# Two plain column-group pairs instead of three ahead of the Strassen pairs, and the right-hand sums one pair earlier

## What is computed

```python
def rmsnorm(x, g):
    xf = x.astype(jnp.float32)
    y = xf * lax.rsqrt(jnp.mean(xf * xf, axis=-1, keepdims=True) + RMS_EPS)
    return (y * g.astype(jnp.float32)).astype(x.dtype)

def swiglu(x, wg, wu, wd):
    return (jax.nn.silu(x @ wg) * (x @ wu)) @ wd

    for l in range(DEPTH):          # DEPTH = 2
        x = x + 0.5 * swiglu(rmsnorm(x, ffn1_norm[l]), ffn1_wg[l], ffn1_wu[l], ffn1_wd[l])
        ...
        x = x + 0.5 * swiglu(rmsnorm(x, ffn2_norm[l]), ffn2_wg[l], ffn2_wu[l], ffn2_wd[l])
    return rmsnorm(x, final_norm)
```

## Time and profile before

| | |
|---|---|
| median of 3 executions | 1958.45 us (1956.9 to 1958.61) |
| the profiled execution, its own time | 1959.18 us |
| its span | 1957.4 us |
| TensorE busy | 1891.2 us (97%) |
| VectorE busy | 1348.5 us (69%) |
| ScalarE busy | 906.3 us (46%) |
| GpSimd busy | 243.1 us (12%) |
| mean granted clock of TensorE | 0.988 of full speed |

### The profile page before, as it was taken

How to read it: one execution, slowest core, us unless ns; L and a number is a source line. 1 busy time by engine, 2 the same in 40 slices (tenths; PEclk the granted TensorE clock), 3 DMA queues, 4 the chain that set the end, 5 groups by cost and what they waited for, 6 DMA issues and landing times.

```text
span 1957.4 us, 31136 instructions
## 1 busy us (share of the span) xinstructions
PE 1891.2 (97%) x11220; PEld 1654.4 (85%) x11220; DVE 1348.5 (69%) x1894; ACT 906.3 (46%) x1521; POOL 243.1 (12%) x208
## 2 busy tenths in 40 slices
PE   6999999998989999999999999999999999999996
PEld 5899988776868889998888999888776788999885
DVE  6789843566779579884357888525785677888424
ACT  4455523427347535553243555324377543555322
POOL 2100000213213210000021000001156221000001
PEclk9999999999989999999999999999999999999998
DMA  4232332322210222323222233332321022333321
GB/s 154 68 121 92 108 128 86 101 87 54 72 60 27 81 87 95 120 86 129 98 79 103 87 107 107 111 104 86 113 72 34 23 77 84 108 107 107 113 102 43
DMA packets 36204, 177.14 MB, mean 91 GB/s; under 512 B 12688, under 2 KB 13072, under 8 KB 15520
## 3 DMA queue, kind: packets, MB, share of 16 engines
q1 hardware_dynamic: 33696, 172.55, 26.0%
q10 hardware_dynamic: 2240, 2.98, 0.4%
q0 software_dynamic: 192, 0.59, 0.1%
HBM read 174.01 MB, written 2.10 MB: 90 GB/s over the span
## 4 chain that ended last, share of the span: by engine, by line
PE 90%; DVE 5%; ACT 2%; POOL 1%; issue 1%; DMA 0%; POOLq 0%; ACTq 0%; DVEq 0%
PE ps L308 29%; PE ps L310 28%; PE ps L309 28%; PE ps L1419 1%; DVE wl L278 1%; DVE xgl L356 1%; ACT wh L274 1%; PE ps L1442 1%; PE ps L1049 1%; POOL xg L2225 1%; DVE small L1005 0%; PE ps L1180 0%; PE ps L997 0%; POOL acc L390 0%; PE ps L979 0%
## 5 line engine op out<-in xcount | busy, mean ns | idle before, releaser
L308 PE MATMUL ps<-xgh,wh 128*128 128x256 f32 (+1 forms) x1504 | 514.7, 342 | 24.2 <-DVE xgl L356 13.8
L310 PE MATMUL ps<-xgh,wl 128*128 128x256 f32 (+1 forms) x1504 | 505.8, 336 | 0.0
L309 PE MATMUL ps<-xgl,wh 128*128 128x256 f32 (+1 forms) x1504 | 505.7, 336 | 0.0
L278 DVE TENSOR_TENSOR wl<-raw,wh 128x2048 fp32r<-128x2048 f32 (+1 forms) x93 | 215.0, 2312 | 355.6 <-ACT wh L274 355.6
L308 PE MATMUL ps<-tmh,wh 128*128 128x256 f32 (+1 forms) x1344 | 414.3, 308 | 0.0
L309 PE MATMUL ps<-tml,wh 128*128 128x256 f32 (+1 forms) x1344 | 414.3, 308 | 0.0
L310 PE MATMUL ps<-tmh,wl 128*128 128x256 f32 (+1 forms) x1344 | 414.3, 308 | 0.0
L274 ACT ACTIVATE wh<-raw 128x2048 fp32r<-128x2048 f32 (+1 forms) x93 | 176.5, 1897 | 356.6 <-PE ps L310 355.4
L308 PEld LDWEIGHTS ps<-xgh,wh 128*128 128x128 f32 x1504 | 286.8, 191 | 60.0 <-issue 18.9
L309 PEld LDWEIGHTS ps<-xgl,wh 128*128 128x128 f32 x1504 | 286.9, 191 | 30.4 <-issue 2.9
L310 PEld LDWEIGHTS ps<-xgh,wl 128*128 128x128 f32 x1504 | 286.6, 191 | 29.7
(11 more groups left out here) (284 smaller groups left out, 2599.8 us busy)
## 6 DMA issues: line engine op xcount, KB each, us to landing
raw<-in_units SPq DMA_DIRECT2D x161, 1024.0 KB, 4.9
x<-in_xT ACTq DMA_DIRECT2D x4, 512.0 KB, 7.7
outT<-x SPq DMA_DIRECT2D x8, 256.0 KB, 2.1
relb<-in_rpb SPq DMA_DIRECT2D x64, 24.0 KB, 2.2
cosA<-in_rope_a ACTq DMA_DIRECT2D x1, 256.0 KB, 2.6
sinA<-in_rope_a ACTq DMA_DIRECT2D x1, 256.0 KB, 2.9
cosD<-in_rope_d POOLq DMA_DIRECT2D x1, 256.0 KB, 3.2
sinD<-in_rope_d POOLq DMA_DIRECT2D x1, 256.0 KB, 3.0
```

Of the source, the lines that this page charges most:

```text
L278: nc.vector.tensor_tensor(wl[:, c % 2, 0:n], raw[:, c % 2, 0:n], wh[:, c % 2, 0:n].bitcast(F32), ALU.subtract).then_inc(w_lo, 1)
L308: nc.tensor.matmul(dst, lh, rh, start=first, stop=False, skip_group_check=onto)
L309: nc.tensor.matmul(dst, lh, rl, start=False, stop=False, skip_group_check=onto)
L310: return nc.tensor.matmul(dst, ll, rh, start=False, stop=last, skip_group_check=onto)
```

## The change

One less plain pair in each of the four blocks and one more pass of the Strassen loop; the four right-hand sums stand at the end of pair 0 in VectorE's queue. With `NS` = 2 the second pair (p == 1) is also the last plain one, so that `sums_hi`, `sums_lo` and the preparation of the first Strassen pair stand in the same pair.

```diff
@@ -47,7 +47,7 @@
-NS = 3
+NS = 2
 RP = PAIRS - NS
 HALF = SEQ // 2
@@ -766,7 +766,6 @@
                 if p == 1:
-                    right_sums(dve, f)
                     for t in range(4):
                         sums_lo(dve, f, t)
                 if p == NS - 1:
@@ -785,6 +784,7 @@
                 if p == 0:
                     for k in range(4, KD):
                         normed(k)
+                    right_sums(dve, f)
             right_lo(dve, f, 1)
```

## The result

The changed kernel takes 1979.24 us (median of 4, 1977.56 to 1980.09) against 1957.68 us of the kernel before (median of 4). The ratio is 1.0108, 95% interval 1.0095 to 1.0120: 1.1% slower. The forecast was 1978 us. The profiled execution has a span of 1978.2 us, 20.8 us more than before.

A forecast was written before the change was run, and what follows sets the result against it. TensorE was taken as the bound, waiting for VectorE's queue ahead of Strassen. 15.8 us lost in the blocks plus 2.8 for the clock made 18.6 on 1959.2, 1977.8; forecast 1978 us, 1976 to 1980, wider range 1970 to 1985.

The forecast's parts named there:

- The sum: Over the four blocks: 15.8 us lost net of the pass plus 2.8 us for TensorE's clock, 18.6 us in all.
- the blocks without the clock: From tg of pair 1 through the added pass: 3.1 us lost in block 1, 12.7 in the other three, together 15.8.
- the clock: TensorE at low clock from j=0 after the longer idle time: 0.7 us a block, 2.8 in all, range 0 to 9.4.
- The gain of the exchange: On TensorE, a Strassen pass of 20.16 us replaces a plain pair of 21.76: 1.60 us a block, 6.4 in all.
- VectorE's chain: VectorE's queue from tg of pair 1 to right_lo of part 1, second block: from 701.24, ending at 718.45.
- bounded at 0 to 0.9 and taken at 0.9: At sums_lo: GpSimd's two products with 1/rms hold VectorE back, starting 3.9 us after tg instead of 3.0.
- its old collision: In the kernel before, left_sum took 1.79 us beside GpSimd's work against 0.68; it was to lose these 1.1 us.
- the 3.4 us of the earlier trace: First block of the kernel before: after 3.86 us idle TensorE ran at half its granted clock for 3.4 us.
- The high bound: From j=0, the low clock lasting twice the row's stretch: 2.4 us a block, 9.4 in all.
- After that nothing is won back: After right_lo of part 1 the same queues follow as before, so the first pass wins back nothing.
- the forecast's rival with the shorter chain: Cover holds at right_lo of part 1: chain ending at 714.3 breaks even; full 6.4 us gain, 1952 to 1953; chance 0.05.

The follow-up runs named there:

- the pair of half changes: Two edits of the changed kernel: three plain pairs with only right_sums moved, 1958.06 us; two plain pairs with right_sums left where it was, 1978.63 us.
- the chain's two reorderings: Changed kernel with two sums_lo deferred behind right_lo of part 2, 1970.88 us; with left_lo of j=2 and j=3 also deferred behind right_lo of part 1, 1972.18 us.
- four plain pairs: Changed kernel with NS = 4 instead of 2, right_sums still at the end of pair 0: 1965.54 us, ratio 1.0034.
- the filled run: Changed kernel with five (first block) or six (others) never-read matmuls filling TensorE's idle time behind the last plain unit: 1973.74 us, ratio 1.0076.
- the run with the move alone: Changed kernel with NS back at 3, so only right_sums is moved to the end of pair 0: 1958.06 us, ratio 0.9995.
- the pieces: Kernel before with part 1 of xn in four pieces of 128x256, product j=1 waiting for one piece per row block: 1958.52 us, ratio 1.0001.
- the copy: Kernel before with part 1 of xn in four pieces and ScalarE's copy of product j=0 ahead of part 2 of xn: 1958.95 us, ratio 1.0005.
- the lightened pass: Kernel before with pieces and copy first, four left_sum of the first Strassen pass cut to 8 of 512 columns (computation incomplete): 1952.81 us, ratio 0.9975.
- the deferred sums: Changed kernel with two sums_lo behind right_lo of part 2, 1970.88 us; the same with two or three filling matmuls, 1973.01 us.
- four low parts deferred: Changed kernel with two sums_lo behind right_lo of part 2 and left_lo of j=2 and j=3 behind right_lo of part 1: 1972.18 us, ratio 1.0078.
- the run with the pairs alone: Changed kernel with right_sums put back behind tg of pair 1, still two plain pairs: 1978.63 us, ratio 1.0103.

## Why the prediction was right

**The place and the mechanism** are shown by the pair of half changes and by the chain's two reorderings: the loss is the missing pair, it sits in VectorE's queue, and two instructions taken out of that queue shorten TensorE's idle time by their 2.2 us. The sum came to 18.6 us and the profiled executions differ by 20.8. Three errors make that up: the blocks without the clock 0.9 us less than said, the clock 1.8 us more, and the mixers, which the sum did not have, 1.3 us more. That they partly cancel is luck.

**The gain of the exchange.** Worked out 1.60 us a block, measured 1.6 with four plain pairs. The figures of the Trainium skill ("TensorE: Matmul & The Clock Gate", "Back-to-back issue gap"), by which it would be 2.4 us, an estimate, or a loss, were left aside for the rows' 227 and 120 ns, and the run agrees with the rows.

**VectorE's chain.** From `tg` of pair 1 to j=0 the sum was 716.0 - 701.24 = 14.8 us; the changed kernel shows 722.70 - 707.98 = 14.72. `sums_lo` begins at 2.93 us and is held for 0.91 us, as bounded at 0 to 0.9 and taken at 0.9; the run without GpSimd's products confirms the cause. `left_sum` took 2.65 us, free of its old collision, as said. The idle time was to be 5.9 us and is 5.65. Without the clock the blocks lose 2.9, 4.0, 4.0 and 4.0 us (the filled run), 14.9 in all; the sum said 15.8.

**The clock** was the term with the wrong size, though small: 0.7 us a block was said, and the filled run puts it at 1.1, 1.3 and 1.6 us in the first three blocks and 0.6 in the fourth, 4.6 us instead of 2.8. (In the fourth the filled kernel is itself at the low clock for the last 3 us, granted 0.50 from 1957.8 on, and the changed one at 1.00, so 0.6 is too little.) The step that was off is the stretch. I took the 3.4 us of the earlier trace rows; in the changed kernel the steps of 0.21 us go on for 5.1, 4.9, 5.7 and 5.5 us in the four blocks (722.70 to the matmul at 727.55 in the second), so j=0 and nearly all of j=1 run slowly. The high bound, twice the row's stretch, held it. The row was one case of several: at the same place, behind nearly the same idle time (3.83 us against 3.86), the low clock lasted 5.8 us in the run with the move alone. A second small error had the other sign: a matmul of 256 columns costs 0.213 us at the low clock, not the doubled 0.24. From 120 ns for 256 columns and 227 for 512, 256 columns more cost 107 ns; 213 is twice that, and why the other 13 ns of the 120 do not appear beside it, no run here shows.

**"After that nothing is won back"** was right for the changed kernel, but for a reason that I had not worked out. I took the first pass as bound by TensorE, since the later passes are the earlier trace rows. It is bound by both: in the filled and the deferred kernels VectorE runs through it from `right_lo` to the third `tg` without a gap above 0.15 us, and the pieces, the copy and the lightened pass show the same limit in the kernel before. This is why the deferred orders end at 3.8 us a block, wherever the wait is put. In the forecast's rival with the shorter chain, an end at 714.3 that is reached by putting work later would therefore not have been enough to break even; no run here takes the work away from the chain altogether.

**What no step held**: the mixers. In the changed kernel's profile they moved by 2.6 and -1.3 us, together 1.3, and in the experiments of the table they lie between -1.0 and 2.6 (even) and between -2.5 and 0.0 (odd), with the time at the low clock. They fell out small here by chance.

## What to carry to other kernels

When a stage that feeds the next is shortened on the bound engine, add up what the other engines must finish under it, in the order of their queues, and compare the end with the new end of the stage; average shares (VectorE was at 69%) say nothing of that. A wait at such a border that vanishes in a timeline can come back inside the next stage, so an order change is worth only what the amount of work up to the next common point allows. An idle time on TensorE costs its length plus a stretch at the low clock, and that stretch is to be measured, not taken as one value. Where another engine is the later one right behind the idle time, the low clock costs nothing more, as with the deferred sums.

## What the runs showed of the hardware

- TensorE was at the low clock behind idle times of 4.53 and 5.65 us in the changed kernel, and back at the high one after 4.9 to 5.7 us of unbroken matmuls, against 3.4 us at its first such place in the kernel before. The length of the idle time does not decide alone: with four low parts deferred the granted clock was 0.64 in the 3.4 us behind an idle time of 2.23 us (second block) and 1.00 behind one of 2.22 us (third block), as the two rows below show. In the even mixer, where matmuls come with gaps, it was at the low level in one kernel and not in another for the same instructions.

```profile
715.60:719.00 3.40, 3.27 (x17) 2.98 (x18) 3.40 (x5) 2.62 (x6) 0.00 (x0) 0.64 0.00 0
1068.30:1072.00 3.70, 2.98 (x22) 2.78 (x23) 3.70 (x7) 3.00 (x6) 0.00 (x0) 1.00 0.00 0
```

- A VectorE tensor_tensor of float32 with both inputs in SBUF took longer by most of a GpSimd instruction on such a pair, in the three places where the two were seen to meet: 1.11 us at `left_sum` before, 0.91 at `sums_lo`, 1.10 at `right_sums` in the run with the pairs alone. It was gone when GpSimd's operation was cut to 8 columns.
- A float32 matmul of 128x512 took 0.86 us in the filled idle time (10 us for twelve), almost four times the 0.23 of one in the shortened format.
